# A six-layer float32 transformer block on one core: small waits rearranged, and the mixed layer's norm, index queries, top-k mask and convolution taps moved

## The chip, the cores and the metric

One core of one Trainium2 chip runs the whole program. The metric is device time in microseconds (us) of one execution. Engines: TensorE (PE) multiplies and transposes, VectorE (DVE) and ScalarE (ACT) work on SBUF and PSUM, GpSimd (POOL) on SBUF alone, and SyncE (SP) issues most of the loads. Each engine runs its own list of instructions in order, and semaphores tie the lists together.

## The reference

Four layers with post-norm (`x = layernorm(ALPHA * x + branch(x))`), their branches latent attention (MLA), windowed attention with sinks (SWA), attention with forget gates (FOX) and MLA again; then one mixed layer, a gated feed-forward (2816 wide) and a last gated projection, these with RMS norms. 512 tokens, 1024 channels, 16 heads of 64, float32 throughout. The mixed layer, on which most of the change lies:

```python
a_in, gate_c, gate_b, ...            # columns of rmsnorm(x) @ w_in
h = gate_c * a_in                    # short convolution: 3 taps over the tokens
y = gate_b * causal_depthwise_conv3(h, conv_w)
sc = relu(einsum("bqhd,bsd->bqhs", iq, ik))          # index scores, 8 heads
score = einsum("bqh,bqhs->bqs", iw, sc) * idx_scale  # masked to s <= t
_, sel = top_k(score, 128)           # keys that each query may attend to
probs = softmax(q . k * scale + bias[rel_bucket], over sel)   # 4 heads
# besides: window means (pooling), and 4 heads of full causal attention
```

All four results are concatenated and go through `w_out_2`.

## The kernel before

**Weights.** `plan_units` cuts all weights into 254 units of up to 1024 columns on 128 partitions, in the order of use. Each goes through a pipe: SyncE loads it into one of 3 raw buffers, ScalarE rounds it to fp32r (`w_hi`, `split(u)`, three units ahead of use, by `advance` or `early`), GpSimd subtracts (`w_lo`), and TensorE forms every product from three fp32r matmuls (`three`: high by high, high by low, low by high). Activations have a high part (ScalarE) and a low part (VectorE) too: `QKh/QKl`, `OTh/OTl`, `XTh/XTl`.

**Groups.** `tile(name)` on TensorE is 24 matmuls of 128x512 into bank 6 or 7; `begin` waits until the group two before has been stored. ScalarE and VectorE count the same groups (`group()`, `stored`). `place` puts a group in another bank.

**Attention.** `pair_attention` exists once on each engine and handles two heads at a time; iteration `i` runs from -2. On TensorE an iteration is `fill(i, 0)`, eight `step`s (transposes of pair `i` and scores of pair `i + 2`), `fill(i, 1)`, `fill(i, 2)`, the last scores, `mix(i)`, `fill(i, 3)`; each `fill` puts projections of later pairs there. ScalarE copies the transposes (`turned`), takes the exponentials (`exps`) and prepares weights; VectorE takes the maxima with the bias (`maxima`) and divides (`norm`). In the last iteration the first three rows of the output projection (`ahead`, `out_ahead`) are woven with the transposes (`weave`).

**Layer tails.** `out_rows` ends the output projection with the token tiles in the order 3, 2, 1, 0 (`ROWS`). VectorE's `ln_tail` makes each tile's layer norm, `turn(n)` transposes it, and ScalarE and VectorE store its halves. Work on the columns of the first tiles is opened meanwhile (`open_half`: tokens 256 to 511 of a tile of weights), and `tile` later finishes it. Before the mixed layer an RMS norm follows each layer norm (`h_norm`).

**The mixed layer.** Its units were, in this order: index keys `ik`, four index queries `iq`, six `conv`, then pool, queries, keys and values. Six `idx_block`s (four heads each, for the query tiles 1 to 3) alternate with the six convolution tiles; ScalarE takes the relu, VectorE the weighted sum into `WORK[t]`. Then `top(n)` does rounds of MAX8 and MATCH_REPLACE8: 16 for each of three query tiles, 48 in all, spread over VectorE's list. The last converts the rest into a mask in `misc`, and `maxima` adds bias and mask for pairs 2 and 3 in two passes. The convolution is done by VectorE: a product (`CONV_H`), three taps (`CONV_Y`), a product (`otmp`). GpSimd computes the window sums of the pooling.

```python
if pr.sel and t:                                     # VectorE, maxima
    link(nc.vector.tensor_tensor(pr.score(b, x, t), o, pr.bias(t, x), ALU.add))
    ins = nc.vector.tensor_tensor_reduce(pr.score(b, x, t), pr.score(b, x, t), SEL[t], ...)
```

## Time and profile before

| | |
|---|---|
| median of 3 runs | 1719.9 us (1717.58 to 1723.01) |
| profiled execution, its own time | 1719.99 us |
| span of the profile | 1718.2 us, 24228 instructions |
| TensorE busy | 1655.5 us (96%) |
| VectorE busy | 792.1 us (46%) |
| ScalarE busy | 768.3 us (45%) |
| GpSimd busy | 595.9 us (35%) |
| mean granted clock of TensorE | 0.997 |
| transfers | 161.17 MB, mean 94 GB/s |

The span goes from the first to the last instruction in the profile; the execution's own time is 1.8 us longer. TensorE's busy time and its idle time make up the span. The other engines' idle time costs nothing by itself. Layers, by TensorE: MLA to about 288 us, SWA to 478, FOX to 780, MLA to 1031, mixed to 1262, feed-forward to 1640, last projection to the end.

### The profile page before, as it was taken

How to read it: one execution, taken by the hardware profiler on the slowest of the kernel's cores; microseconds unless marked ns; L12 is line 12 of the kernel's file. 1: busy time of each engine (PE TensorE's matmuls, PEld its weight loads, DVE VectorE, ACT ScalarE, POOL GpSimd, SP SyncE). 2: the span in 40 equal slices, each digit the busy share in tenths (PEclk: the TensorE clock that was granted, in tenths of full speed). 3: DMA queues.
4: the chain of work that ended last, by engine and by line, in shares of the span. 5: the costliest groups of instructions: out<-in, count | busy, mean ns of one | idle time of the engine just before them, and what ended most of it. 6: DMA issues, size and time to landing. Idle time of an engine off the chain costs nothing.

```text
span 1718.2 us, 24228 instructions
## 1 busy us (share of the span) xinstructions
PE 1655.5 (96%) x9321; PEld 1345.2 (78%) x9321; DVE 792.1 (46%) x2055; ACT 768.3 (45%) x1565; POOL 595.9 (35%) x286
## 2 busy tenths in 40 slices
PE   7999999999999999999999998998899999999998
PEld 6777779787788787778777778776688888887877
DVE  2777626566343434426777635889332111000052
ACT  4467634566243545524566634336743222212252
POOL 4323133332243323224322224372134444444423
PEclk9999999999999999999999999999999999999999
DMA  6322144223452322144222146431143333333312
GB/s 167 68 44 62 60 148 140 76 60 66 148 155 75 84 53 77 55 152 110 58 49 76 50 142 178 106 84 53 49 147 111 98 97 95 102 95 91 123 62 86
DMA packets 216046, 161.17 MB, mean 94 GB/s; under 512 B 53755, under 2 KB 197147, under 8 KB 215932
## 3 DMA queue, kind: packets, MB, share of 16 engines
q1 hardware_dynamic: 205904, 130.21, 27.2%
q10 hardware_dynamic: 9804, 29.38, 5.5%
q8 instruction: 75, 1.23, 0.3%
q0 software_dynamic: 224, 0.03, 0.1%
q14 instruction: 39, 0.32, 0.1%
HBM read 148.32 MB, written 11.14 MB: 93 GB/s over the span
## 4 chain that ended last, share of the span: by engine, by line
PE 65%; DVE 10%; ACT 5%; issue 1%; ACTq 0%; POOL 0%; DVEq 0%
PE banks L474 18%; PE banks L476 18%; PE banks L475 18%; PE banks L717 4%; PE banks L686 3%; PE banks L732 3%; ACT AB L1434 1%; DVE misc L2555 1%; ACT G L1558 1%; DVE misc L2542 1%; DVE top L2554 1%; ACT w_hi L1304 1%; ACT AB L1460 1%; DVE QKl L1978 1%; PE banks L875 1%
## 5 line engine op out<-in xcount | busy, mean ns | idle before, releaser
L2717 POOL TENSOR_TENSOR w_lo<-w_raw,w_hi 128x1024 fp32r<-128x1024 f32 (+3 forms) x253 | 573.3, 2275 | 1095.6 <-ACT w_hi L1304 1087.4
L474 PE MATMUL banks<-XTh,w_hi 128*128 128x512 f32 (+4 forms) x1216 | 451.7, 371 | 14.3 <-DVE w_lo L2438 3.7
L475 PE MATMUL banks<-XTl,w_hi 128*128 128x512 f32 (+4 forms) x1216 | 446.0, 367 | 0.0
L476 PE MATMUL banks<-XTh,w_lo 128*128 128x512 f32 (+4 forms) x1216 | 445.8, 367 | 0.0
L1304 ACT ACTIVATE w_hi<-w_raw 128x1024 fp32r<-128x1024 f32 (+3 forms) x254 | 251.0, 996 | 154.6 <-PE banks L476 108.6
L474 PEld LDWEIGHTS banks<-XTh,w_hi 128*128 128x128 f32 (+1 forms) x1216 | 229.5, 189 | 60.4 <-issue 18.3
L476 PEld LDWEIGHTS banks<-XTh,w_lo 128*128 128x128 f32 (+1 forms) x1216 | 229.5, 189 | 38.3
L475 PEld LDWEIGHTS banks<-XTl,w_hi 128*128 128x128 f32 (+1 forms) x1216 | 229.8, 189 | 35.9
L474 PE MATMUL banks<-w_hi,OTh 128*128 128x512 f32 (+1 forms) x448 | 172.2, 384 | 1.8 <-DVE QKl L1978 1.8
L476 PE MATMUL banks<-w_hi,OTl 128*128 128x512 f32 (+1 forms) x448 | 167.8, 375 | 0.0
L475 PE MATMUL banks<-w_lo,OTh 128*128 128x512 f32 (+1 forms) x448 | 167.6, 374 | 0.0
L1460 ACT ACTIVATE AB<-banks 128x512 f32<-128x512 f32 (+1 forms) x200 | 98.7, 528 | 148.7 <-PE banks L717 146.3
L1434 ACT ACTIVATE AB<-AB,nb 128x256 f32<-128x256 f32 (+3 forms) x288 | 152.7, 537 | 13.7 <-DVE nb L2140 10.8
L2634 DVE TENSOR_TENSOR otmp<-banks,AB 128x512 f32<-128x512 f32 x22 | 15.2, 692 | 276.3 <-PE banks L476 276.3
L2130 DVE CUSTOM_DVE_ANT_0 AB<-banks,zmask 128x384 f32<-128x384 f32 (+1 forms) x192 | 83.9, 486 | 82.5 <-PE banks L717 80.0
L2159 DVE TENSOR_SCALAR_CACHE_REDUCE AB<-AB,ri 128x256 f32<-128x256 f32 (+3 forms) x256 | 118.2, 518 | 2.3
L1978 DVE TENSOR_TENSOR QKl<-banks,QKh 128x512 fp32r<-128x512 f32 (+2 forms) x80 | 54.3, 682 | 117.3 <-ACT QKh L1333 116.0
L717 PE MATMUL banks<-ident,AB 128*128 128x128 f32 x672 | 98.1, 281 | 8.6 <-ACT AB L1460 5.8
L474 PEld LDWEIGHTS banks<-w_hi,OTh 128*128 128x128 f32 x448 | 84.3, 188 | 20.2 <-DVE QKl L1978 4.0
L717 PEld LDWEIGHTS banks<-ident,AB 128*128 128x128 f32 x672 | 73.6, 141 | 29.2 <-issue 17.5
L476 PEld LDWEIGHTS banks<-w_hi,OTl 128*128 128x128 f32 x448 | 84.3, 188 | 15.4
L475 PEld LDWEIGHTS banks<-w_lo,OTh 128*128 128x128 f32 x448 | 84.4, 188 | 13.8
(204 smaller groups left out, 2322.4 us busy)
## 6 DMA issues: line engine op xcount, KB each, us to landing
w_raw<-in_w_gate_up_dram SPq DMA_DIRECT2D x44, 512.0 KB, 3.8
w_raw<-in_fox_w_in_dram SPq DMA_DIRECT2D x30, 512.0 KB, 4.1
w_raw<-in_mla_w_in_dram SPq DMA_DIRECT2D x26, 512.0 KB, 4.7
w_raw<-in_w_in_dram SPq DMA_DIRECT2D x24, 512.0 KB, 3.9
w_raw<-in_w_down_dram SPq DMA_DIRECT2D x22, 512.0 KB, 3.5
w_raw<-in_swa_w_in_dram SPq DMA_DIRECT2D x20, 512.0 KB, 3.8
w_raw<-in_mla_w_out_dram SPq DMA_DIRECT2D x16, 512.0 KB, 3.6
x_spill<-AB ACTq DMA_DIRECT2D x16, 512.0 KB, 2.8
```

What stands on the lines that cost most here:

```text
L474: nc.tensor.matmul(o, ah, bh, start=first, stop=False, skip_group_check=True)
L475: nc.tensor.matmul(o, ah, bl, start=False, stop=False, skip_group_check=True)
L476: return nc.tensor.matmul(o, al, bh, start=False, stop=last, skip_group_check=True)
L686: mm = nc.tensor.matmul(bank[2 * (c.sch % 2) + x][:, cols], qp[r, pr.q, ts], kp[r, pr.k, ks], start=n == 0 and t == pr.s_chunks[ch][0], st ...
L717: mm = nc.tensor.transpose(bank[4 + c.tch % 2][:, o:o + P], SBP[a % 2][x][:, col:col + P], ident[:, :])
L1304: nc.scalar.activation(view(w_hi, u, RING), view(w_raw, u, RAW), ACT.Copy).then_inc(hi_done, 1)
L1434: ins = nc.scalar.activation(sc, sc, ACT.Exp, bias=nb[:, b, n0 + t:n0 + t + 1], scale=pr.scale, accum_out=rs[:, b, n0 + t:n0 + t + 1])
L1460: nc.scalar.activation(PTP[x][:, pr.pt[js[0]]:pr.pt[js[0]] + width], bank[4 + c.tch % 2][:, 0:width], ACT.Copy).then_inc(pt_free, 1)
L1978: return nc.vector.tensor_tensor(dst, src, h.bitcast(F32), ALU.subtract)
L2130: ins = nc.vector.tensor_tensor_reduce(pr.score(b, x, t), o, pr.bias(t, x), 1.0, -3e38, ALU.add, ALU.max, mx[:, b, 4 * x + t:4 * x + t + 1])
L2159: ins = nc.vector.tensor_scalar(pr.score(b, x, t), pr.score(b, x, t), ri[:, b, 4 * x + t:4 * x + t + 1], None, ALU.mult, ALU.add, accum_ou ...
L2717: pool.tensor_tensor(view(w_lo, u, RING), view(w_raw, u, RAW), view(w_hi, u, RING).bitcast(F32), ALU.subtract).then_inc(lo_done, 1)
```

## The change

- Start: TensorE does 16 transposes of the identity before the first weight matmul. The seven small constants are no longer loaded by GpSimd at its start, but one behind each of its first weight preparations, the two norm gains first, with a semaphore of their own.
- SWA: the relative bias product stands between the halves of the first value projection; the query tile of pair 1 follows the first pair's scores, and the first gate precedes the second pair's.
- FOX: the rope tables of the second MLA layer are loaded in iterations 3 to 6 and not at the layer's start; ScalarE prepares a weight unit behind the next pair's first exponentials and no longer right behind the values; VectorE takes the second norm behind the mix where values follow.
- Last iteration of every attention: the remaining transpose groups are spread over four places in the second and third output row.
- Tail into the mixed layer: the third token tile's RMS norm comes ahead of the fourth tile's last passes, and its transposes ahead of the opened index-key tile; three index-query tiles are finished before the fourth tile's transposes. Loads for the pooling are issued behind the first index block.
- Convolution: product as before; the taps and the low parts are done by GpSimd between weight preparations, with `CONV_A` as its temporary.
- Attention of the mixed layer: query tiles at `fill(i, 0)` and key tiles at `fill(i, 1)`; the last values in two halves; each query tile's mask is written as NEG or 0 in fp32r (`SEL_R`) as soon as its rounds end, and TensorE adds it to the scores by a matmul with the identity. The order of the score chunks of these pairs is (2, 0), (1), (3).
- Feed-forward: of the two copies of the partial sum VectorE does one.

```diff
-    for i in range(8):
+    tile("gate", swa, D + 512)
+    tile("q", swa, 2 * P)
+    for i in range(1, 8):
...
+    for i in range(3):
+        tile("iq", w_in, iq + i * P)
     units.append(("ik", KD, HD + IDX_HEADS, [(None, 0, HD, reads(w_in, ik, ik + HD)),
...
-    for i in range(4):
-        tile("iq", w_in, iq + i * P)
+    tile("iq", w_in, iq + 3 * P)
...
             def early_mixed(turn):
-                open_half("ik")
                 for _ in range(3):
                     open_half("iq", P)
                 turn(2)
+                open_half("ik")
+                pe.wait_ge(xt_lo, c.xt)
+                for _ in range(3):
+                    tile("iq", n0=P)
                 turn(3)
...
+                    if pr.sel:                                  # TensorE, scores
+                        pe.wait_ge(ident_round, 1)
+                        pe.wait_ge(sel_done, max(pr.s_chunks[ch]))
...
+                        if pr.sel and t:
+                            for x in range(2):
+                                mm = nc.tensor.matmul(bank[2 * (c.sch % 2) + x][:, cols], ident_r[:, :], SEL_R[t],
+                                                      start=False, stop=True, skip_group_check=True)
...
                     if i == n_pairs - 1:
+                        todo = [n for n, ch in ((0, 0), (1, 1), (3, 2), (4, 0), (6, 1), (7, 2)) if ch < len(pairs[i].t_chunks)]
+                        points = [4]
...
+                    for half in range(2):
+                        half_step(k, t, half, src, begun[k], k == 0, False)
+                        if half if k == 1 else t == 0:
+                            weave()
...
             turn_start(1)
+            for _ in range(16):
+                nc.tensor.transpose(bank[0][:, 0:P], ident[:, :], ident[:, :])
             pe.wait_ge(xt_lo, 4)
...
             def fill(i, pos):                                   # TensorE, SWA
-                if pos == 0 and i == -2:
-                    pair_tile("q", 1)
-                elif pos == 1 and -1 <= i < 5:
+                if pos == 1 and i < 5:
                     pair_tile("q", i + 3)
-                elif pos == 2 and -1 <= i < 7:
+                elif (pos == 2 and 0 <= i < 7) or (pos == 0 and i == -1):
                     tile("gate")
...
+                if n == 3:                                      # ScalarE, conv tiles
+                    act.wait_ge(conv_s, 4)
...
-            pair_attention(fox_pairs(), fill)                   # VectorE
+            pair_attention(fox_pairs(), fill, FOX_VALUES)
...
+                    if t not in rounds:                         # VectorE, top
+                        nc.vector.tensor_scalar(SEL_R[t], WORK[t], TAKEN / 2, NEG, ALU.is_gt, ALU.mult).then_inc(sel_done, 1)
...
-                link(nc.vector.tensor_scalar(CONV_Y, CONV_H[:, 0:512], conv_w[:, cc, 0:1], None, ALU.mult))
-                for tap in (1, 2):
-                    link(nc.vector.scalar_tensor_tensor(CONV_Y, CONV_H[:, tap:tap + 512], conv_w[:, cc, tap:tap + 1], CONV_Y,
-                                                        ALU.mult, ALU.add))
...
+            def conv_taps(cc):                                  # GpSimd
+                pool.wait_ge(cst, N_CST)
+                groups_stored(pool, mark["conv", cc])
+                pool.tensor_scalar(CONV_Y, CONV_H[:, 0:512], conv_w[:, cc, 0:1], None, ALU.mult)
+                for tap in (1, 2):
+                    pool.tensor_scalar(CONV_A, CONV_H[:, tap:tap + 512], conv_w[:, cc, tap:tap + 1], None, ALU.mult).then_inc(conv_s, 1)
+                    pool.wait_ge(conv_s, 4 * cc + 2 * tap - 1)
+                    pool.tensor_tensor(CONV_Y, CONV_Y, CONV_A, ALU.add).then_inc(conv_s, 1)
+                    pool.wait_ge(conv_s, 4 * cc + 2 * tap)
```

VectorE, tail into the mixed layer, from the third token tile's layer norm on, before (`banks` holds the layer's output, `HT` tiles lie in `AB`):

```order
L2250 SCALAR_TENSOR_TENSOR banks<-AB,banks 128x1024
L2251 BN_STATS st<-banks 128x6
L2252 BN_STATS st<-banks 128x6
L2253 BN_AGGR mv<-st 128x2
L2256 SCALAR_TENSOR_TENSOR banks<-banks,mv,AB 128x1024
L2017 RECIPROCAL inv<-dev 128x1
L2258 SCALAR_TENSOR_TENSOR AB<-banks,inv,AB 128x1024
L2017 RECIPROCAL inv<-dev 128x1
L2237 SCALAR_TENSOR_TENSOR AB<-AB,inv,V 128x1024
L2017 RECIPROCAL inv<-dev 128x1
L2237 SCALAR_TENSOR_TENSOR AB<-AB,inv,V 128x1024
L2223 TENSOR_TENSOR XTl<-banks,XTh 128x4x128 x4
```

and now:

```order
L2314 SCALAR_TENSOR_TENSOR banks<-AB,banks 128x1024
L2315 BN_STATS st<-banks 128x6
L2316 BN_STATS st<-banks 128x6
L2317 BN_AGGR mv<-st 128x2
L2091 RECIPROCAL inv<-dev 128x1
L2301 SCALAR_TENSOR_TENSOR AB<-AB,inv,V 128x1024
L2323 SCALAR_TENSOR_TENSOR banks<-banks,mv,AB 128x1024
L2091 RECIPROCAL inv<-dev 128x1
L2325 SCALAR_TENSOR_TENSOR AB<-banks,inv,AB 128x1024
L2287 TENSOR_TENSOR XTl<-banks,XTh 128x4x128 x2
L2091 RECIPROCAL inv<-dev 128x1
L2301 SCALAR_TENSOR_TENSOR AB<-AB,inv,V 128x1024
```

The RMS norm of the third tile (the first pass with `V`, the gain) has moved ahead of the fourth tile's two last passes, and the third tile's low part ahead of the fourth's norm.

GpSimd, the mixed layer's start, before (`L2717` is the weight preparation, `L2697` begins the window sums):

```order
L2717 TENSOR_TENSOR w_lo<-w_raw,w_hi 128x576
L2717 TENSOR_TENSOR w_lo<-w_raw,w_hi 128x1024 x14
L2697 TENSOR_TENSOR AB<-AB 128x512 x2
L2705 TENSOR_TENSOR AB<-AB,V 64x512
L2706 TENSOR_TENSOR AB<-AB 64x512
L2705 TENSOR_TENSOR AB<-AB,V 64x512
L2706 TENSOR_TENSOR AB<-AB 64x512
L2717 TENSOR_TENSOR w_lo<-w_raw,w_hi 128x1024 x3
L2697 TENSOR_TENSOR AB<-AB 128x512 x4
```

and now:

```order
L2817 TENSOR_TENSOR w_lo<-w_raw,w_hi 128x576
L2817 TENSOR_TENSOR w_lo<-w_raw,w_hi 128x1024 x6
L2800 TENSOR_SCALAR AB<-AB,conv_w 128x512
L2802 TENSOR_SCALAR AB<-AB,conv_w 128x512
L2804 TENSOR_TENSOR AB<-AB 128x512
L2802 TENSOR_SCALAR AB<-AB,conv_w 128x512
L2804 TENSOR_TENSOR AB<-AB 128x512
L2817 TENSOR_TENSOR w_lo<-w_raw,w_hi 128x1024 x2
L2810 TENSOR_TENSOR OTl<-otmp,OTh 128x512
L2817 TENSOR_TENSOR w_lo<-w_raw,w_hi 128x1024
L2800 TENSOR_SCALAR AB<-AB,conv_w 128x512
L2802 TENSOR_SCALAR AB<-AB,conv_w 128x512
```

Of the ten tap operations the first five and the first low part are seen between weight preparations; the window sums moved behind the second five.

VectorE, mixed attention, from the last top-k round to the maxima of pair 2, before:

```order
L2554 MAX top<-misc 128x8
L2555 MATCH_REPLACE misc<-top,misc 128x512
L2615 TENSOR_SCALAR misc<-misc 128x1152
L2155 RECIPROCAL ri<-rs 128x4 x2
L2126 TENSOR_TENSOR AB<-banks,G 128x384
L2127 ISA AB,mx<-AB,misc 128x384
L2127 ISA mx 128x1
L2130 ISA AB,mx<-banks,G 128x128
L2130 ISA mx 128x1
```

and now:

```order
L2634 MAX top<-misc 128x8
L2635 MATCH_REPLACE misc<-top,misc 128x512
L2637 TENSOR_SCALAR OTh<-misc 128x512
L2052 TENSOR_TENSOR QKl<-banks,QKh 128x512
L2199 ISA AB,mx<-banks,G 128x384
L2199 ISA mx 128x1
L2199 ISA AB,mx<-banks,G 128x128
L2199 ISA mx 128x1
```

The conversion of all three tiles became one of the last tile, the low part of a query tile stands ahead of the maxima, the wait for pair 1's exponentials (the two RECIPROCAL) is no longer ahead of them, and one pass over the scores replaces two.

## Rows read from the trace of the kernel before

**Rows 1.** view of waits, TensorE, whole span: engine, line, releaser, us in total, times, longest

```profile
PE banks L875 <- DMA AB<-in_x_dram: 6.1, 2, 5.2
...
PE banks L474 <- DVE G L2363: 0.3, 2, 0.2
```

**Rows 2.** TensorE in order of time, start: start us, us, engine, line, operation, [idle before]

```profile
8.06 1.97 PE L875 MATMUL banks<-ident,AB 128*128 128x128 f32 x8 [0.90 <-DMA AB<-in_x_dram]
13.77 0.55 PE L474 MATMUL banks<-XTh,w_hi 128*128 128x256 f32 x1 [3.74 <-DVE w_lo L2438]
...
18.12 0.28 PE L476 MATMUL banks<-XTh,w_lo 128*128 128x256 f32 x1
...
21.36 0.28 PE L476 MATMUL banks<-XTh,w_lo 128*128 128x256 f32 x1
```

**Rows 3.** view of waits, TensorE, 298 to 316 us

```profile
PE banks L686 <- DVE mx L2130: 2.0, 2, 1.6
PE banks L474 <- ACT V_odd L1760: 1.2, 1, 1.2
```

**Rows 4.** TensorE in order of time, mixes of last pairs

```profile
228.97 2.38 PE L732 MATMUL banks<-AB,V_odd 128*64 128x512 f32 x16 [0.83 <-ACT AB L1460]
...
437.88 1.74 PE L732 MATMUL banks<-AB,V 128*64 128x256 f32 x16 [0.67 <-ACT AB L1460]
```

**Rows 5.** TensorE in order of time, third layer

```profile
492.77 0.47 PE L474 MATMUL banks<-XTh,w_hi 128*128 128x512 f32 x1 [1.26 <-ACT AB L1793]
...
705.14 0.36 PE L474 MATMUL banks<-w_hi,XTh 128*128 128x256 f32 x1 [0.84 <-DVE G L2011]
...
719.10 1.11 PE L717 MATMUL banks<-ident,AB 128*128 128x128 f32 x6 [1.34 <-ACT AB L1460]
```

**Rows 6.** ScalarE in order of time, behind the third layer's last values

```profile
717.42 1.05 ACT L1304 ACTIVATE w_hi<-w_raw 128x1024 fp32r<-128x1024 f32 x1
```

**Rows 7.** busy by stretch: PE, PEld, DVE, ACT, POOL with counts; clock, DMA, GB/s

```profile
722.00:723.00 1.00, 1.00 (x4) 0.71 (x4) 0.55 (x1) 1.00 (x4) 0.00 (x0) 0.50 0.81 262
...
1186.00:1187.00 1.00, 1.00 (x7) 0.67 (x6) 0.97 (x3) 0.39 (x1) 0.00 (x0) 0.50 0.00 0
```

**Rows 8.** view of waits, TensorE, 1035 to 1072 us

```profile
PE banks L1119 <- DVE QKl L1978: 1.4, 1, 1.4
PE banks L875 <- DVE AB L2237: 1.4, 2, 0.8
```

**Rows 9.** view of waits, TensorE, 1110 to 1150 us

```profile
PE banks L474 <- DVE otmp L2577: 1.6, 1, 1.6
PE banks L1128 <- issue: 0.5, 1, 0.5
```

**Rows 10.** view of waits, TensorE, 1150 to 1243 us

```profile
PE banks L686 <- DVE QKl L1978: 4.1, 2, 2.4
PE banks L732 <- DVE QKl L1978: 2.8, 1, 2.8
PE banks L717 <- ACT AB L1460: 2.5, 3, 1.5
PE banks L717 <- ACT AB L1449: 1.7, 1, 1.7
```

**Rows 11.** VectorE's line of the index sums: duration ns min/median/max, first and last start

```profile
L2542 DVE SCALAR_TENSOR_TENSOR misc<-AB,iw_t,misc x21: 483/619/2724, 1072.7 to 1116.4; 128x256 f32<-128x256 f32 x7, 128x384 f32<-128x384 f32 x7, 128x512 f32<-128x512 f32 x7
```

**Rows 12.** GpSimd's groups by shape: busy us, mean ns, idle before

```profile
L2697 POOL TENSOR_TENSOR AB<-AB 128x512 f32<-128x512 f32 x6 | 6.5, 1081 | 0.6 <-issue 0.3
...
L2678 POOL COPY w_raw<-w_raw 128x128 f32<-128x128 f32 x2 | 0.6, 287 | 1.0 <-DMA w_raw<-in_mla_w_in_dram 1.0
```

**Rows 13.** VectorE's groups by shape, 1035 to 1053 us

```profile
L2258 DVE SCALAR_TENSOR_TENSOR AB<-banks,inv,AB 128x1024 f32<-128x1024 f32 x2 | 2.6, 1284 | 0.1
```

**Rows 14.** VectorE in order of time, last selection

```profile
1192.81 0.76 DVE L2615 TENSOR_SCALAR misc<-misc 128x1152 f32<-128x1152 f32 x1
```

**Rows 15.** TensorE in order of time, second feed-forward part

```profile
1552.46 0.50 PE L474 MATMUL banks<-XTh,w_hi 128*128 128x512 f32 x1 [1.18 <-ACT V L1944]
```

327 lines of the change are left out of this document (198 added, 129 removed).

## The prediction

> **What bounds the kernel now.** I read the page first, then the view of waits of TensorE over the whole span, then TensorE's rows in order of time around every wait above 0.2 us, and only then the other engines around those places. TensorE is busy nearly throughout; its waits are small and many. The view of waits has 24 groups, from 6.1 us down to 0.3 us [rows 1], and they sum to 56.3 us of a 1718.2 us span. So this kernel's time is TensorE's work plus this list, and a change that removes no TensorE work can return at most some 56 us plus what a low clock costs. The reader is to see that no single wait matters, and that the change must be priced wait by wait.
>
> Three more stretches are slow without a wait: right after the waits at 719, 1052 and 1185 us the granted clock is 0.50, TensorE's lower level [rows 7] (the first and the last of the three). Each lasted 3.4 us at half speed, so each cost 1.7 us. In each case TensorE had stood still for 1.6 us or more within the few microseconds before it [rows 5, 8, 10]; but other waits of this size are not followed by one, so the clock's part is less sure than the waits.
>
> **The change, part by part.** I go along the span; gains are positive.
>
> Start. The first weight matmul begins at 13.77 us after 3.74 us of idling, and the first 20 matmuls take (18.12 - 13.77) / 20 = 0.218 us each, the later ones (21.36 - 18.12) / 27 = 0.120 us [rows 2]: 20 x 0.098 = 1.9 us. The 16 added transposes go into the idle stretch. Eight took 1.97 us there [rows 2], so 16 need 3.5 to 3.9 us against a gap of 3.74 us: they fill it and may overrun by 0.2. I take 1.8. Bounds: -0.3 (they overrun and the clock is no higher) to 2.9 (the constants' transfers, no longer beside the first tokens, also give a microsecond). The moved DMA issues stand behind weight preparations on GpSimd's queue; the gains are needed only in the latent scaling and the others in the second layer.
>
> Second layer. The two matmuls of the relative bias now stand between the halves of the value projection: of the 1.2 us wait on their copy [rows 3] 0.2 should stay. The 2.0 us before the second pair's scores [rows 3] get a query tile and a gate tile as cover. But the second query tile is then directly before the first transposes: the next scores need its low half (about 1.5 us after the tile), and VectorE divides the first pair's second half (1.9 us) only behind it. I expect 0.8 and 1.1 us of new wait there, so this cover gives nothing net. Sum 1.0; bounds -1 to 3.
>
> Third layer. Eight rope-table issues leave ScalarE's queue ahead of the value copies: 1.26 us go [rows 5] (its first row). They return two at a time where ScalarE waits for matmuls anyway. VectorE now normalises behind the mix where values follow: the gate tile's wait of 0.84 goes. In the 1.34 us wait after the last values ScalarE did a weight split of 1.05 us ahead of the copy that TensorE waited for [rows 5, 6]; it now comes after: 1.0. With it the low clock behind it should go, 1.7. Sum 4.8; bounds 2.1 to 5.1.
>
> Last pair of each layer. The last two transpose groups stood back to back ahead of the mix, which waited 0.83 us in four layers and 0.67 in the windowed one [rows 4]. Now six output matmuls stand behind the last transposes: 4 x 0.83 + 0.67 = 4.0; bounds 2 to 4.
>
> Tail into the mixed layer. Before, TensorE waited 1.4 us for the two normalised token tiles and 1.4 us for the index queries [rows 8]. Now the third tile's norm runs ahead of two passes of 1.28 us each [rows 13] over the fourth, so it is ready about 2.8 us earlier; but TensorE also comes 2.9 us earlier, since one opened tile (24 matmuls at 0.12) now stands behind that turn: about 0.9 of wait, and 0.1 for its low half. The wait on the fourth tile's low half stays, for nothing is between its turn and its use. The second 1.4 go, because three query tiles end a tile earlier and ScalarE's five DMA issues stand behind the first index block. So 2.8 becomes 1.0: 1.8, and 1.7 for the clock: 3.5; bounds 0 to 5.
>
> Convolution and pooling. VectorE loses two taps and a low part per half; GpSimd gains three TENSOR_SCALAR and two TENSOR_TENSOR of 512 columns. The latter take 1.08 us; a COPY of a quarter of the columns took 0.28 [rows 12], so a TENSOR_SCALAR lies between 0.3 and 1.1; I take 1.0, near the row of equal width: 5.2 us per half. What counts is VectorE's accumulations beside it. They take 0.48 us at best and 2.72 at worst [rows 11]; the worst spans a weight preparation on GpSimd: an operation with both inputs in SBUF stands still meanwhile, while the top-k operations do not.
> The Trainium skill, "SBUF — State Buffer" (section "SBUF: two separate sides"), says that VectorE and GpSimd share a port pair as an exclusive lock, and the loser "fully blocks". By that rule each tap operation can hold up an accumulation; the trace agrees, with the 2.72 us above.
> From the stretched accumulations alone I count only part of the taps' use: idle sum before 1.6 [rows 9] + 0.5 for the pool product + 0.3 = 2.4. After: 0.7 before the fifth index block (ScalarE's relu waits for the convolution product behind three top-k rounds), 1.3 where 1.6 was, 1.5 for the pool product, whose GpSimd chain has one low part of 1.08 more ahead, 0.4 for the second: 3.9. So -1.5; bounds -9 (rival A) to 2.4. Queued behind GpSimd's new waits is the preparation of the next weights, needed only two tiles of 5.6 us later.
>
> Mixed attention. The waits were 4.1, 2.8, 2.5 and 1.7 = 11.1 us [rows 10]. Each of the first got a projection tile as cover: query tiles are now before the scores and key tiles behind. The 2.8 (a bank held by VectorE's late low part behind the masked maxima) goes, for that part is now ahead of the maxima; the 1.7 goes with the exponentials done first under the second value half. The next late thing is ScalarE after the first mix, about 1.0, and the six transposes of the third pair in a row, about 1.3. So 11.1 - 2.3 = 8.8. The mask costs TensorE 12 matmuls, 4 x (256 + 384 + 512) = 4608 columns at 0.12 us per 256: -2.1. Low clock gone: 1.7. VectorE's last selection ended at 1192.81 + 0.76 [rows 14]; scores of 512 keys now wait for it. By the order after it should come some 3 us before TensorE asks, so nothing; without that margin every microsecond counts in full. Sum 8.4; bounds 2 to 12.
>
> Feed-forward. One of the two copies goes to VectorE, so they overlap: of 1.18 [rows 15] 0.4 goes.
>
> Sum: 1.8 + 1.0 + 4.8 + 4.0 + 3.5 - 1.5 + 8.4 + 0.4 = 22.4 us. The profiled execution took 1719.99 us, the median of the runs shown is 1719.9, so both give 1697.6.
>
> **The rivals.**
> A. GpSimd's taps hold VectorE up as its weight preparations do. Ten tap operations of 1.08 us can hold VectorE for 10.8 us; 1.5 are counted. For it: accumulations did stretch to 2.72 us. Against: VectorE has idle time before index blocks, and the top-k rounds are unaffected. If 7 more reach TensorE: 1704.6.
> B. The low clock stays or falls in new places, as in the second layer where I foresee two new waits within 3 us. Three such stretches: 22.4 - 5.1 = 17.3, so 1702.7.
> C. The waits that I added (1.9 second layer, 3.9 convolution, 2.3 attention) come out mostly hidden; 6 of 8.1 us less: 1691.6.
> D. Slower: GpSimd's TENSOR_SCALAR with a scale per partition is far slower than the rows allow me to think; no row shows one. Six stand in a chain whose product holds ScalarE's relu and so the next index block. Each microsecond above 1.0 costs six, so above 4.7 us each the whole gain is gone. At 6 us: 1697.6 + 30 = about 1727.
> E. The change moves waits rather than removing them, and nothing is left: ScalarE and VectorE are each half idle and their order alone decides the rest; a new wait behind each removed one gives 1718.
>
> **How the numbers follow.** Forecast 0.58, A 0.18, B 0.08, C 0.09, D 0.04, E 0.03. What a measurement here can tell from no change is 0.3%, 5.2 us. Forecast, A, B and C are faster by more: 0.93; E is the same: 0.03; D is slower: 0.04. The range takes in A, B and C with their spread: below, 1689, since every bound above together is unlikely; above, 1709, where A and B meet. Outside it lie D, E and a little of A.
>
> **What would show it.** Start: the matmuls from about 13.8 us are 0.12 apart. Waits before the mixes of the last pairs are gone; in the third layer no wait above 0.5 us between 485 and 745. Granted clock 1.0 behind the third layer's last values and between 1040 and 1190. GpSimd's TENSOR_SCALAR at about 1 us (D falls above 2). A new wait in the second layer before the third pair's scores, and waits of 3 to 4 us in the convolution. The scores of 512 keys with a mask start without waiting for VectorE. I am wrong if the waits' sum stays above 40 us, if the mask's matmuls are far longer than 0.24 us, or if weights come late.

## The result, and the profile after

The changed kernel takes 1699.1 us (1696.4 to 1700.9, four runs), the kernel before 1720.8 us in the same comparison: ratio 0.9877, interval 0.9862 to 0.9891. That is 21.8 us less; the forecast was 1697.6, in a range of 1689 to 1709. A second set of runs of the same changed kernel gave 1699.3 us (1697.1 to 1701.1), ratio 0.9882 (0.9864 to 0.9900).

| | before | after |
|---|---|---|
| profiled execution | 1719.99 us | 1696.41 us |
| span | 1718.2 us | 1694.3 us |
| TensorE busy | 1655.5 us | 1654.3 us |
| sum of TensorE's waits, by the view of waits | 56.4 us | 33.4 us |
| VectorE busy | 792.1 us | 785.9 us |
| GpSimd busy | 595.9 us | 613.0 us |

The profiled execution is the fastest of the four. TensorE does the same work plus 12 mask matmuls and the 16 transposes of the start, and its waits sum to 23.0 us less: the time is again its work plus its waits.

TensorE's waits over the whole span of the changed kernel (line waited for, releaser, us in total, times, longest; 13 groups left out) answer to [rows 1]:

```profile
PE banks L905 <- DMA AB<-in_x_dram: 5.2, 1, 5.2
PE banks L739 <- ACT AB L1510: 3.5, 9, 0.6
...
PE banks L905 <- DVE AB L2301: 2.1, 3, 1.1
PE banks L481 <- DVE XTl L2287: 2.0, 3, 1.6
PE banks L1133 <- DVE QKl L2052: 1.8, 1, 1.8
...
PE banks L1161 <- issue: 1.7, 1, 1.7
...
PE banks L481 <- DVE otmp L2654: 0.3, 1, 0.3
```

Of before, the waits at L686 and L732 (4.1 and 2.8 us, [rows 10]) and the one of 1.6 on `otmp` [rows 9] are gone or small. Two are not: the 1.4 us at the index scores (L1119, [rows 8]) are 1.8 now, at the small transposes ahead of them (L1133), and the 0.5 at the pool product (L1128, [rows 9]) are 1.7 (L1161). What is left in one piece are the first tokens (5.2 us), the tail into the mixed layer (1.1 + 1.6 + 1.8 us) and the pool product (1.7 us).

The start, TensorE in order of time, answers to [rows 2]. The first weight matmul begins 1.96 us earlier, and the next ones are 0.12 us apart at once:

```profile
8.62 2.07 PE L1019 MATMUL banks<-ident 128*128 128x128 f32 x16
11.81 0.36 PE L481 MATMUL banks<-XTh,w_hi 128*128 128x256 f32 x1 [1.12 <-DVE w_lo L2515]
12.01 0.28 PE L482 MATMUL banks<-XTl,w_hi 128*128 128x256 f32 x1
```

Granted clock (the third number from the right) in the changed kernel, against [rows 7]. While TensorE works, one low stretch is left, in the tail (a second one begins at 1691.7 us, behind the last matmul); where the third of before was, it is 1.00:

```profile
1047.00:1050.00 3.00, 3.00 (x16) 3.00 (x15) 1.11 (x2) 1.51 (x3) 3.00 (x2) 0.50 0.50 117
1185.00:1189.00 4.00, 3.47 (x31) 2.58 (x28) 1.47 (x5) 2.74 (x7) 0.00 (x0) 1.00 0.00 0
```

How far each part moved TensorE's work, read as the start of the same matmuls in both profiles (before minus after, then the difference from one place to the next):

| part | places (before / after, us) | forecast | measured |
|---|---|---|---|
| start | 41.63 / 37.80 | 1.8 | 3.8 |
| rest of the first layer | 256.46 / 251.70 | 0.8 | 0.9 |
| second layer | 464.74 / 457.73 | 1.7 | 2.3 |
| third layer | 769.76 / 756.70 | 5.6 | 6.0 |
| fourth layer, tail, to the first index scores | 1071.06 / 1057.20 | 4.3 | 0.8 |
| convolution, to the first pool product | 1131.42 / 1117.39 | -1.5 | 0.2 |
| mixed attention, to the feed-forward's start | 1285.87 / 1262.29 | 9.2 | 9.5 |
| feed-forward | 1552.46 / 1528.47 | 0.4 | 0.4 |
| sum | | 22.4 | 23.9 |

(The last pairs' 4.0 us are spread over the layers where they lie.) Two rows are off by 2 us or more, in opposite ways (start and tail), and the convolution by 1.7; the sum hides that.

The tail, TensorE in order of time: the third token tile's transposes, the fourth's, the index keys behind them, and the small transposes ahead of the first index scores.

```profile
1031.73 1.09 PE L905 MATMUL banks<-ident,AB 128*128 128x128 f32 x8 [1.05 <-DVE AB L2301]
...
1043.74 1.06 PE L905 MATMUL banks<-ident,AB 128*128 128x128 f32 x8
1046.37 0.34 PE L481 MATMUL banks<-XTh,w_hi 128*72 128x256 f32 x1 [1.57 <-DVE XTl L2287]
...
1056.95 0.32 PE L1133 MATMUL banks<-ident,AB 8*128 8x8 f32 x3 [1.83 <-DVE QKl L2052]
```

GpSimd's groups by shape (busy us, mean ns, idle before), against [rows 12]: a TENSOR_SCALAR takes 1.71 us where 1.0 was taken, a tap's addition 1.34.

```profile
L2802 POOL TENSOR_SCALAR AB<-AB,conv_w 128x512 f32<-128x512 f32 x4 | 6.8, 1712 | 0.2
L2779 POOL TENSOR_TENSOR AB<-AB 128x512 f32<-128x512 f32 x6 | 6.5, 1084 | 0.3
L2804 POOL TENSOR_TENSOR AB<-AB 128x512 f32<-128x512 f32 x4 | 5.4, 1341 | 0.3
...
L2800 POOL TENSOR_SCALAR AB<-AB,conv_w 128x512 f32<-128x512 f32 x2 | 3.5, 1730 | 5.3 <-DVE AB L2646 3.1 <-issue 2.2
```

VectorE's accumulations of the index scores, against [rows 11]:

```profile
L2622 DVE SCALAR_TENSOR_TENSOR misc<-AB,iw_t,misc x21: 483/750/2778, 1059.2 to 1097.6; 128x256 f32<-128x256 f32 x7, 128x384 f32<-128x384 f32 x7, 128x512 f32<-128x512 f32 x7
```

By shape their sum rose from 17.2 us (6.3 + 5.6 + 5.3) to 21.7 us (7.7 + 7.6 + 6.4). Little of this stands beside the taps: the four accumulations that overlap a tap operation are longer than their shape's shortest by 0.9 us and three times 0.24 us, 1.6 us in all. The four that overlap a weight preparation are longer by 7.1 us (before: two, by 4.2 us).

### The profile page after: what moved, and what is told of

Same layout as the page of the kernel before. It is cut to its first block, busy times and chain, and to the rows that moved or that the text cites. A ratio compares the mean times of both kernels' runs of the same rounds, so it can differ in the third digit from the quotient of the medians.

```text
span 1694.3 us, 24289 instructions
## 1 busy us (share of the span) xinstructions
PE 1654.3 (98%) x9349; PEld 1343.5 (79%) x9349; DVE 785.9 (46%) x2038; ACT 767.5 (45%) x1565; POOL 613.0 (36%) x298
## 4 chain that ended last, share of the span: by engine, by line
PE 81%; DVE 9%; ACT 6%; issue 2%; POOL 1%; DMA 0%; ACTq 0%; SPq 0%; DVEq 0%; POOLq 0%
PE banks L481 22%; PE banks L483 22%; PE banks L482 22%; PE banks L739 5%; PE banks L700 4%; PE banks L754 4%; PE banks L905 1%; PE banks L723 1%; ACT G L1613 1%; ACT AB L1484 1%; ACT w_hi L1354 1%; DVE misc L2622 1%; DVE AB L2228 1%; POOL w_lo L2817 1%; DVE QKl L2052 1%
## 5 line engine op out<-in xcount | busy, mean ns | idle before, releaser
L2817 POOL TENSOR_TENSOR w_lo<-w_raw,w_hi 128x1024 fp32r<-128x1024 f32 (+2 forms) x253 | 572.3, 2271 | 1050.6 <-ACT w_hi L1354 1039.4
L481 PE MATMUL banks<-XTh,w_hi 128*128 128x512 f32 (+5 forms) x1216 | 450.7, 371 | 7.2 <-DVE XTl L2287 2.0
L483 PE MATMUL banks<-XTh,w_lo 128*128 128x512 f32 (+5 forms) x1216 | 444.7, 366 | 0.0
L482 PE MATMUL banks<-XTl,w_hi 128*128 128x512 f32 (+5 forms) x1216 | 444.7, 366 | 0.0
L1354 ACT ACTIVATE w_hi<-w_raw 128x1024 fp32r<-128x1024 f32 (+4 forms) x254 | 250.3, 995 | 160.3 <-PE banks L483 107.7
L481 PEld LDWEIGHTS banks<-XTh,w_hi 128*128 128x128 f32 (+2 forms) x1216 | 228.2, 188 | 53.2 <-issue 11.2
L483 PEld LDWEIGHTS banks<-XTh,w_lo 128*128 128x128 f32 (+2 forms) x1216 | 228.2, 188 | 38.1
L482 PEld LDWEIGHTS banks<-XTl,w_hi 128*128 128x128 f32 (+2 forms) x1216 | 228.4, 188 | 36.1 <-issue 0.2
```

The costliest lines, as they stand in the source:

```text
L481: nc.tensor.matmul(o, ah, bh, start=first, stop=False, skip_group_check=True)
L482: nc.tensor.matmul(o, ah, bl, start=False, stop=False, skip_group_check=True)
L483: return nc.tensor.matmul(o, al, bh, start=False, stop=last, skip_group_check=True)
L1354: nc.scalar.activation(view(w_hi, u, RING), view(w_raw, u, RAW), ACT.Copy).then_inc(hi_done, 1)
L2817: pool.tensor_tensor(view(w_lo, u, RING), view(w_raw, u, RAW), view(w_hi, u, RING).bitcast(F32), ALU.subtract).then_inc(lo_done, 1)
```

## Experiments

Each is the changed kernel with one thing undone or added, unless said; medians beside 1699.1 and 1699.3 us.

**Is the low clock fixed in its places?** The changed kernel once more, without an edit.

> The changed kernel once more, unchanged, beside the next two, as their measure. Its first profile has a wait of 1.83 us before the index scores and a low clock behind the 1.57 us wait before it; five variants that leave this place alone show 2.9 to 3.3 us there and the low clock behind it, and three runs show a low clock at 320 us that it does not have. Theory: these two places change from execution to execution (the low clock of 1.7 us falls or does not), which is the spread of 1696.4 to 1700.9: here one of them or both differ from the first profile. Rival: they are fixed, and the variants' edits made them: the profile repeats 1.83 us and no low clock at 320 and 1060 us.

Measured: 1699.3 us, and another profile, of the slowest of its runs (1701.1 us, span 1699.0). The low clock now lies at 321.3 to 324.7 us and at 1058.6 to 1065.4 us, and no longer at 1046.6 to 1050.0:

```profile
322.00:323.00 1.00, 1.00 (x10) 0.78 (x7) 0.00 (x0) 0.00 (x0) 0.00 (x0) 0.50 0.07 19
1059.00:1060.00 1.00, 1.00 (x10) 0.98 (x11) 0.32 (x2) 0.19 (x1) 1.00 (x1) 0.50 1.10 236
1063.00:1064.00 1.00, 1.00 (x4) 0.81 (x3) 0.00 (x0) 0.00 (x0) 0.00 (x0) 0.50 1.08 269
```

```profile
1048.00 0.34 PE L481 MATMUL banks<-XTh,w_hi 128*72 128x256 f32 x1 [1.57 <-DVE XTl L2287]
...
1058.67 0.45 PE L1133 MATMUL banks<-ident,AB 8*128 8x8 f32 x3 [3.26 <-DVE QKl L2052]
```

So the same kernel has low stretches in other places from execution to execution, and the wait ahead of the index scores is 3.3 us where no low clock stood before it: in the first profile the 3.4 us at half speed had brought TensorE there 1.4 us later. From the 1.57 us wait to the small transposes it is 10.6 us in the first profile and 10.7 in the second, so the low stretch between them cost next to nothing: the wait behind it became shorter by what it took. The theory holds. Elsewhere a stretch of 3.4 or 6.8 us costs up to half of its length. The profile of 1694.3 us was a lucky one: its execution is the fastest of the eight of this kernel, and two profiles of the same kernel differ by 4.7 us of span. A forecast from one profiled execution (three stretches) to another has an uncertainty of some 2 us from this, either way, by my estimate.

**The start, two runs.** `after_cold` leaves out the 16 transposes; `before_warm` is the kernel before with them alone.

```diff
-            for _ in range(16):
-                nc.tensor.transpose(bank[0][:, 0:P], ident[:, :], ident[:, :])
```

> The changed kernel without its 16 transposes at the start. The start gained 3.8 us where 1.8 was forecast: the first weight matmul begins 1.96 us earlier, and its matmuls are 0.12 instead of 0.22 us apart. Theory: two independent parts, the earlier begin from the constants' transfers that no longer stand beside the first tokens, the spacing from the transposes. Then here the first weight matmul still begins at about 11.8 us, about 19 matmuls are 0.21 us apart, and the time is 1.9 us more than the changed kernel's 1699.1: 1701.0. Rival: with the idling cut from 3.7 to some 3 us the matmuls come at full speed by themselves: spacing 0.12 from the start, 1699.

> The kernel before with nothing but the 16 transposes. Theory: the first weight matmul begins at 13.8 us as before (the transposes fit into the idling), its matmuls are 0.12 us apart, gain 1.9 us: 1718.9 against 1720.8. Rival: the transposes end some 1.6 us before the weights are there, TensorE stands still again, and the first matmuls are 0.21 us apart as before: no gain, 1720.8.

Measured: `after_cold` 1701.6 us, `before_warm` 1719.2 against 1720.7 us (ratio 0.9992, 0.9981 to 1.0003, by itself not told from no change). The profiles tell what the times can't. Without the transposes, the first weight matmul still begins at 11.9 us, and the first 22 take 4.82 us, 0.22 each; from there 0.12:

```profile
11.90 0.55 PE L481 MATMUL banks<-XTh,w_hi 128*128 128x256 f32 x1 [2.98 <-DVE w_lo L2513]
...
16.51 0.37 PE L481 MATMUL banks<-XTh,w_hi 128*128 128x256 f32 x1
...
17.08 0.28 PE L482 MATMUL banks<-XTl,w_hi 128*128 128x256 f32 x1
```

In the kernel before with them, the first weight matmul begins at 13.61 us, 2.15 us after the last transpose, and its followers are 0.12 us apart:

```profile
9.55 1.91 PE L989 MATMUL banks<-ident 128*128 128x128 f32 x16
13.61 0.36 PE L474 MATMUL banks<-XTh,w_hi 128*128 128x256 f32 x1 [2.15 <-DVE w_lo L2440]
```

Both theories hold for the transposes: they give 1.9 to 2.1 us. The earlier first matmul does not come from them; of the other edits only the constants' transfers lie ahead of it, but no run moves them alone. Nor does a pause of 2.15 us bring the low speed back there. The other traces bear this out: in each, the clock's own record begins, at full speed, where the matmuls' spacing halves. That is at 18.1 and 16.7 us in the two without the transposes, and at 8.5 to 12.0 us in the twelve with them. The moment differs from execution to execution, so the transposes themselves took 1.9 to 3.3 us; in `before_warm` the speed had risen at 9.24 us, just before them, and they kept TensorE at work in what had been a pause of 3.74 us.

**The last pairs.** `after_no_weave` puts the transpose groups back to back again.

```diff
-                        todo = [n for n, ch in ((0, 0), (1, 1), (3, 2), (4, 0), (6, 1), (7, 2)) if ch < len(pairs[i].t_chunks)]
-                        points = [4]
...
-                            if len(todo) >= points[0]:
+                            if todo:
                                 step(i, todo.pop(0))
...
-                        if half if k == 1 else t == 0:
-                            weave()
+                    weave()
```

> The changed kernel with the last pairs' transposes as before (back to back behind the first rows, ahead of the mix). Theory: the waits before the mixes return, 0.83 us in four layers and 0.67 in the windowed one, 4.0 us in all: 1703.1. Rival: the waits were only put elsewhere, and the woven order has cost something of its own: waits return but others go, under 2 us: 1700.

Measured: 1703.9 us (1703.7 to 1704.1). TensorE's waits of this line were 0.6 us in the changed kernel; here, 0.83 us four times and 0.67 once beside it:

```profile
PE banks L754 <- ACT AB L1505: 4.6, 6, 0.8
```

4.0 us came back in this view, as the theory says; the medians are 4.6 to 4.8 us apart, so up to a microsecond lies elsewhere.

**The third layer.** `after_fox_early_split` prepares the weight unit right behind the values again.

```diff
-                elif pos == 5 and i - 1 in FOX_VALUES:
-                    advance()
-                    early()
...
-                        advance()
-                        for half in range(2):
-                            values(half, FOX_VALUES[i] % 2)
+                        value_units(FOX_VALUES[i] % 2)
```

> The changed kernel, but in the third layer ScalarE prepares the next weight unit right behind the values again, ahead of the copy of transposes that TensorE waits for. Theory: the wait behind the last values grows from 0.39 to about 1.4 us, the granted clock falls to 0.50 behind it for 3.4 us (1.7 us of cost): 2.7 us more than 1699.1: 1701.8. Rival: only the wait returns and the clock stays at 1.00, since the two never hung together: 1700.1. Second rival: the exponentials that are now ahead of it cover the preparation: no change.

Measured: 1700.6 us. The wait is back, 1.34 instead of 0.39 us, and behind it the clock is low from 711.7 to 715.1 us:

```profile
709.52 1.60 PE L739 MATMUL banks<-ident,AB 128*128 128x128 f32 x10 [1.34 <-ACT AB L1510]
```

```profile
713.00:714.00 1.00, 1.00 (x4) 0.81 (x3) 0.50 (x1) 1.00 (x5) 0.00 (x0) 0.50 0.93 369
```

In this layer the two cost 2.5 us (633.92 to 759.35 us here, 633.77 to 756.70 in the changed kernel). The theory holds by the profile. The median moved by 1.2 to 1.5 us only. The other low stretches can explain the rest: the mean granted clocks of its four executions average 0.9978, those of the changed kernel 0.9970 and 0.9973, which at 1700 us is an estimated 0.9 to 1.3 us in this variant's favour.

**The taps.** `after_dve_taps` gives them back to VectorE; ScalarE's wait for them goes too.

```diff
+                groups_stored(dve, c.g)
+                link(nc.vector.tensor_scalar(CONV_Y, CONV_H[:, 0:512], conv_w[:, cc, 0:1], None, ALU.mult))
+                for tap in (1, 2):
+                    link(nc.vector.scalar_tensor_tensor(CONV_Y, CONV_H[:, tap:tap + 512], conv_w[:, cc, tap:tap + 1], CONV_Y,
+                                                        ALU.mult, ALU.add))
                 idx_block(3 * cc + 2)
...
-                dve.wait_ge(conv_s, 4 * cc + 4)
...
-                if u in (conv0 + 4, conv0 + 7):
-                    conv_taps((u - conv0 - 4) // 3)
```

> The changed kernel with the convolution's taps done by VectorE again (product, then TENSOR_SCALAR and two accumulations, ahead of the third index block of each half); the low parts stay with GpSimd. VectorE gets 7.3 us of work back. In the changed kernel the last selection ends at 1177.2 us and the scores of 512 keys start at 1179.4: 2.2 us of slack. Theory: taps on GpSimd are worth what they take off VectorE ahead of the last selection: a part falls into VectorE's idle time, the selection ends 3 to 6 us later and TensorE waits 1 to 4 us before the scores of 512 keys; waits of 1 to 2 us before the index blocks return: 1703 (1700 to 1706). Rival A of the prediction: GpSimd's taps stretch VectorE's accumulations (21.7 us in sum against 17.2 before), so that VectorE gains little; with the taps back they are short again and the time is 1698 to 1700.

Measured: 1706.1 us (1706.0 to 1707.2), 0.1 us above the theory's range, and not by its path. TensorE did not wait for the selection; it waited in the convolution (view of waits, 1070 to 1136 us), with a low clock behind each wait:

```profile
PE banks L481 <- DVE otmp L2656: 2.5, 1, 2.5
PE banks L1152 <- ACT AB L1940: 2.3, 1, 2.3
```

```profile
1093.00:1094.00 1.00, 1.00 (x4) 0.83 (x3) 1.00 (x1) 0.89 (x2) 1.00 (x1) 0.50 0.00 0
1117.00:1118.00 1.00, 1.00 (x4) 0.81 (x3) 0.93 (x4) 0.97 (x2) 1.00 (x1) 0.50 0.00 0
```

2.3 + 2.5 + 0.4 us in place of 0.3 + 1.7 are 3.2 us more, two low stretches 3.4: together 6.6, of 6.8 measured. (Its other two low stretches, at 321 and 1058 us, stand in the second profile of the changed kernel as well.) So the taps on GpSimd are worth 6.8 us in the changed kernel. That is not a gain over before: this row of the table moved by 0.2 us. Between the convolution's two products VectorE now does six and four top-k rounds where it did one; without the taps moved, the new order would have cost some 6.6 us here (an estimate, 6.8 less 0.2). Rival A of the prediction is right in a small part: the accumulations sum to 19.1 us here (9.2 + 6.5 + 3.4) against 21.7. Of these 2.6 us some 1.6 stood beside the taps; the rest is weight preparations that meet other accumulations. VectorE is rid of 7.3 us by the taps, and no wait shows that the 1.6 us reached TensorE. Rival D is out: at 1.71 us a TENSOR_SCALAR stands far below the 4.7 us from which it would have decided.

**The mask.** `after_dve_mask` adds it on VectorE in a second pass.

```diff
-                            for x in range(2):
-                                mm = nc.tensor.matmul(bank[2 * (c.sch % 2) + x][:, cols], ident_r[:, :], SEL_R[t],
-                                                      start=False, stop=True, skip_group_check=True)
...
+                                link(nc.vector.tensor_tensor(pr.score(b, x, t), o, pr.bias(t, x), ALU.add))
+                                ins = nc.vector.tensor_tensor_reduce(pr.score(b, x, t), pr.score(b, x, t), SEL_R[t].bitcast(F32), 1.0, -3e38,
```

> The changed kernel with the top-k mask added by VectorE again, in a second pass over the scores (12 more passes), without the mask's 12 matmuls and without TensorE's wait for the selection. Theory: TensorE gives back 2.1 us, but the maxima of the last two pairs come 2 to 3 us later each and TensorE waits for exponentials and banks: 1702 (1699 to 1705). Rival: the new order of the query and key tiles did it all, and the mask on TensorE is a pure loss of 2.1 us: 1697.

Measured: 1701.6 us. TensorE is rid of 2.1 us of matmuls and waits 2.77 us for VectorE's maxima before the scores of 512 keys, 1.03 us where it was 0.46, and 1.7 us go to a low clock from 1184.0 to 1187.4 us:

```profile
1183.02 0.50 PE L700 MATMUL banks<-QKh 64*128 64x512 f32 x2 [2.77 <-DVE mx L2198]
...
1191.04 1.11 PE L732 MATMUL banks<-ident,AB 128*128 128x128 f32 x6 [1.03 <-ACT AB L1503]
```

2.8 + 0.6 + 1.7 - 2.1 = 3.0 us, where 2.3 to 2.6 were measured. The mask on TensorE pays, by some 2 us net. The rest of the 9.5 us I put down to the order, to the last pair (0.8) and to the low clock that is gone (1.7); no run undoes the order by itself.

**The tail, four runs.** `tail_turn` moves the fourth tile's transposes ahead of the third finished query tile:

```diff
-                for _ in range(3):
+                for _ in range(2):
                     tile("iq", n0=P)
                 turn(3)
+                tile("iq", n0=P)
```

> The changed kernel with the fourth token tile's transposes ahead of the third of the finished index-query tiles and no longer behind it. In the changed kernel that tile's norm is ready at 1037.4 us and its transposes start at 1043.7; TensorE then waits 1.57 us for its low half and the clock is 0.50 for 3.4 us. Theory: the query tile of 2.7 us covers the low half, the wait and the low clock both go: 1.6 + 1.7 = 3.3 us less than 1699.1: 1695.8. Rival: the wait goes but the clock falls behind the next wait of this size (1.83 us, ten us later): 1697.5.

Measured: 1695.6 us (1693.7 to 1695.9). The 1.57 us went, and so did the low clock in the tail; but the wait ahead of the index scores is 2.92 us:

```profile
1056.10 0.32 PE L1134 MATMUL banks<-ident,AB 8*128 8x8 f32 x3 [2.92 <-DVE QKl L2053]
```

`best1` has this edit and two more: ScalarE's copy of the index keys ahead of `advance()`, and `conv_low(1)` behind `window_sums(0)`.

```diff
             act.wait_ge(xt_lo, c.xt)
-            advance()
             o = group()
...
+            advance()
...
-                elif u in (conv0 + 6, conv0 + 9):
-                    conv_low((u - conv0 - 6) // 3)
+                elif u == conv0 + 6:
+                    conv_low(0)
                 if u == pool0 + 3:
                     window_sums(0)
+                    conv_low(1)
```

> The changed kernel with three edits: the fourth token tile's transposes ahead of the third finished index-query tile; ScalarE copies the index keys ahead of the weight preparation that it now does first (it waits there until 1052.5 us while the keys are ready at 50.8); GpSimd does the second low part of the convolution behind the window sums, for whose result TensorE waits 1.71 us. Theory: 3.3 us for the first, 1.8 for the second (the wait before the first index block), 1.3 for the third (one low part): 6.4 us less than 1699.1: 1692.7. Rival: the waits at the index block and at the pool product are set by VectorE's low parts and by the window sums' own length, and only the first edit pays: 1695.8.

Measured: 1695.2 us, no more gained than by `tail_turn`: the rival's time. The keys are now there in time (1052.49 us, no wait), and the wait stands one group further on, 2.56 us:

```profile
1052.49 0.35 PE L1134 MATMUL banks<-ident,AB 8*128 8x8 f32 x3
...
1056.30 0.59 PE L481 MATMUL banks<-XTh,w_hi 128*128 128x512 f32 x1 [2.56 <-DVE QKl L2053]
```

So the keys' copy alone was not the cause. The third edit did shorten the first pool product's wait, from 1.71 to 0.50 us, but 0.74 us came up at the second, so 0.5 us is left of the 1.3 expected. ScalarE's weight preparations waited for loads. SyncE's own rows in the changed kernel show why: it issues four loads from 1020 to 1027 us, stands until 1046.4 us at `wait_ge(xt_lo, mark["mixed"])`, the last token tile's low part, and then puts four bias rows, 1.8 to 2.0 us together, ahead of each load:

```profile
1020.12 6.97 SPq L1327 DMA_DIRECT2D w_raw<-in_w_in_dram  x4
1046.41 1.76 SPq L1311 DMA_DIRECT2D G<-rel_scratch  x4
1048.22 0.42 SPq L1327 DMA_DIRECT2D w_raw<-in_w_in_dram  x1
1048.69 1.97 SPq L1311 DMA_DIRECT2D G<-rel_scratch  x4
```

The load of 1048.22 us landed at 1052.42 and is what ScalarE prepares at 1052.49, ahead of the keys' copy:

```profile
1052.49 1.06 ACT L1354 ACTIVATE w_hi<-w_raw 128x1024 fp32r<-128x1024 f32 x1 [3.98 <-issue]
1053.58 0.59 ACT L1926 ACTIVATE AB<-banks 8x512 f32<-8x512 f32 x1
```

`bias_late` is the changed kernel with that wait and the bias rows two units later, and nothing else:

```diff
-                if u == conv0:
+                if u == conv0 + 2:
                     sp.wait_ge(rel_dma, 16 * 8)
                     sp.wait_ge(xt_lo, mark["mixed"])
-                if conv0 <= u < conv0 + 8:
-                    bias_rows(u - conv0)
+                if conv0 + 2 <= u < conv0 + 10:
+                    bias_rows(u - conv0 - 2)
```

> The changed kernel, but SyncE's wait for the last token tile's halves, and the 32 issues of bias rows that stand between its weight loads, come two weight units later. In the changed kernel SyncE stands from 1027 to 1046.4 us at that wait, the next weight load is issued at 1048.2 us and ScalarE's preparation of it, at 1052.5, holds up the copy of the index keys. Theory: that load is what the 1.8 to 3.3 us before the index scores wait for: they go (to under 0.5 us), the 1.57 us stay: 2 to 4 us less, 1696 (1695 to 1697.5). Rival: the keys' own copies (0.6 + 1.2 us on ScalarE, 1.4 on VectorE) behind 4 us of cover set it: nothing changes, 1699.

Measured: 1694.9 us (1694.3 to 1695.5), 4.2 to 4.5 us less and 0.1 us below the theory's range. SyncE issues six loads before the first bias row, the one that was held back now at 1028.2 us, and no wait above 0.45 us is left between 1047 and 1115 us; the 1.57 us and the low clock behind it stay:

```profile
1020.21 29.54 SPq L1327 DMA_DIRECT2D w_raw<-in_w_in_dram  x6
1049.87 1.89 SPq L1311 DMA_DIRECT2D G<-rel_scratch  x4
```

The theory holds: a load that SyncE held back is what the wait ahead of the index scores hung on. In the kernel before SyncE stood at the same place. Its first bias rows and the load behind them, which landed at 1058.4 us, are shown here; whether its own wait of 1.4 us hung on that load, no run shows.

```profile
1052.61 1.75 SPq L1261 DMA_DIRECT2D G<-rel_scratch  x4
1054.40 0.43 SPq L1277 DMA_DIRECT2D w_raw<-in_w_in_dram  x1
```

**All together.** `best2` joins `best1` and `bias_late`, and swaps the first gate with the third query tile of the second layer.

```diff
-    tile("gate", swa, D + 512)
     tile("q", swa, 2 * P)
+    tile("gate", swa, D + 512)
...
-                if pos == 1 and i < 5:
+                if (pos == 1 and i < 5 and i != -1) or (pos == 0 and i == -1):
                     pair_tile("q", i + 3)
```

> All together on the changed kernel: the fourth token tile's transposes ahead of the third finished index-query tile; the index keys' copy ahead of the weight preparation; SyncE's wait and bias rows two units later; GpSimd's second low part behind the window sums; and in the second layer the third query tile ahead of the first gate, so that its low half is not needed right behind it (0.77 and 0.87 us of waits there, with a low clock of 1.7 us in some runs). Theory: before the index scores no wait above 0.5 us, no low clock between 1030 and 1070 us: 3.3 + 2.5 us; pool product 1.2; second layer 1.2 and the low clock: 8 us less than 1699.1: 1691. Rival: in the tail the earlier finish only meets the next thing (best1 turned 1.57 + 1.83 us into 2.56 us and gained no more than its first edit alone): 1694 to 1695.

Measured: 1693.3 us (1691.7 to 1694.6). In the tail no wait is left between the fourth tile's transposes and the index scores, and no low clock, as the theory says; the 1.1 us before the third tile's transposes stay. At the pool products 1.7 us became 0.5 + 0.7, a gain of 0.5 where 1.2 was expected. The swap went wrong: 0.77 + 0.87 us became one wait of 2.52 us, with a low clock behind it.

```profile
321.23 0.66 PE L740 MATMUL banks<-ident,AB 128*128 128x128 f32 x4 [2.52 <-DVE AB L2229]
```

`best3` is `best2` without the swap.

> The last kernel without its edit in the second layer (the gate goes ahead of the third query tile again, as in the changed kernel): there the waits of 0.77 and 0.87 us had become one of 2.52 us with a low clock behind it. What stays are the four edits of the tail and the convolution. Theory: 0.9 us less than 1693.3 by the waits, and up to 1.7 more where no low clock falls at 320 us: 1692 (1691 to 1693). Rival: the low clock at 320 us falls behind 0.77 and 0.87 us as well, as in some runs of the changed kernel, and the tail's gain is the whole: no difference that can be told from 1693.3.

Measured: 1691.2 us (1690.8 to 1692.8), ratio to before 0.9837 (0.9819 to 0.9855): 8 us below the changed kernel, 29 below the one before. The 0.77 and 0.87 us are back, and this execution has no low stretch before TensorE's last matmul. It is 2.1 us below `best2`, of which 0.9 are the waits; but the two were measured in different comparisons and their ranges touch, so how much the low clock at 320 us adds is not shown. The largest waits left between 1018 and 1140 us:

```profile
PE banks L906 <- DVE AB L2302: 1.1, 1, 1.1
PE banks L1162 <- POOL AB L2789: 0.7, 1, 0.7
PE banks L1162 <- issue: 0.5, 1, 0.5
```

## Why the prediction was right, and where it was wrong

*Bound by TensorE's work and its waits*: right. Waits 23.0 us less, low stretches 3.4 (three against one) and the start's low speed 1.9 less, the mask 2.1 and the 16 transposes 2.1 more: 24.1, of 23.9 measured.

*Start*: too small, 3.8 against 1.8, outside its upper bound of 2.9. The transposes gave what was said (1.9 to 2.1: `after_cold` by its profile and its median, `before_warm` by its profile). They did not fill the gap, though: the price of 3.5 to 3.9 us was taken from transposes at the low speed, and here they took 2.07 us, since the speed rose among them. The moved constants were given at most "a microsecond" and gave 1.96: before, the second token tile came 0.9 us late [rows 2] and ScalarE waited 0.65 us more for the first weights, whose preparation began at 11.31 us; in the changed kernel neither waits and it begins at 9.36.

*Second layer*: right in its parts, 2.3 against 1.7; of the wait on the copy nothing stayed, where 0.2 were left. The new waits of 0.77 and 0.87 us stand where 0.8 and 1.1 were forecast, and there the low clock falls in some executions, as rival B had it.

*Third layer*: right, 6.0 against 5.6 with the last pair's. The clock's share, of which I was less sure, came back in `after_fox_early_split`'s profile together with the wait.

*Last pairs*: right, 4.0 us by the waits that come back when they are undone.

*Tail*: wrong. The step that failed is "the second 1.4 go, because three query tiles end a tile earlier and ScalarE's five DMA issues stand behind the first index block". 3.5 us were forecast and nothing came (6.08 us of waits and clock before, 6.15 after). The issues on ScalarE were not what was last: a weight load was, held back by SyncE's wait for the last token tile, which I had not looked up in SyncE's own rows. `bias_late` moved that wait and the bias rows behind it, and gave 4.2 to 4.5 us. The first part of the step (0.9 us of wait before the third tile) came as 1.05, and the wait on the fourth tile's low part stayed as said, but so did the low clock behind it, which the forecast had let go.

*Convolution*: better than forecast, 0.2 against -1.5. GpSimd's operations cost more (1.71 and 1.34 us for 1.0 and 1.08), the chain of a half is 7.8 us for 5.2, yet the waits forecast ahead of the fifth index block (0.7), of the convolution product (1.3) and of the second pool product (0.4) came as 0, 0.3 and 0; only the first pool product's did, 1.7 for 1.5. I had left out that VectorE, rid of 7.3 us, reaches its product earlier than the longer chain is late: at the first product it did not wait for GpSimd, at the second 0.46 us.
The Trainium skill, "GPSIMD Engine Reference" (section "3.1 Elementwise — side-by-side cycle accounting"), gives 769 ns as the best case of a loop over 512 elements and puts TENSOR_TENSOR above it, for its two inputs. Here it is the other way: 1.71 us with one input and a scale per partition (1.55 the shortest), 1.08 us with two inputs [rows 12], and the measurement decides.

*Mixed attention*: right in sum, 9.5 against 9.2 with the last pair's 0.8. The waits left are 0.46, 0.39, 0.29 and 0.56 us, 1.7 where 2.3 were forecast. The margin of the selection was 3.0 us, as estimated: VectorE's last selection began at 1176.79 us and took 0.43, and TensorE needs it only for the mask behind the scores of 512 keys, at 1180.26 (the expectation of `after_dve_taps`, which says 2.2, counts to the scores themselves):

```profile
1176.79 0.43 DVE L2637 TENSOR_SCALAR OTh<-misc 128x512 fp32r<-128x512 f32 x1
```

```profile
1179.37 0.50 PE L700 MATMUL banks<-QKh 64*128 64x512 f32 x2
...
1180.26 0.73 PE L717 MATMUL banks<-OTh,ident_r 128*128 128x512 f32 x2
```

*Rivals*: A is out as a loss, though the accumulations did grow by 4.5 us, 1.6 of them beside taps. B was partly true: low stretches still fall, one of 3.4 us in the first profile of the changed kernel, 3.4 and 6.8 us in the second. The eight executions of this kernel take 1696.4 to 1701.1 us, and the forecast of 1697.6 lies within them. That the sum came so near is partly luck: the start's 2.0 and the convolution's 1.7 us more than forecast made up for the tail's 3.5 less. C was partly true: of the 8.1 us of new waits 5.3 came (1.6 in the second layer, 2.0 in the convolution, 1.7 in the attention). D and E are out.

## What to carry to other kernels

Price a change by the list of single waits and the low clock behind them, but for each wait follow all queues that feed it, the load queue's own waits too: a wait that was put down to VectorE's copy hung on a weight load that SyncE had held back for 19 us. A cover removes a wait only when nothing else is nearly as late; `best1` moved the wait one group further, at 2.6 us, and gained nothing by it until the load was early. And a low stretch that lies ahead of a wait is paid for by that wait; only one with no wait close behind it costs its half. Compare low-clock stretches between two profiles before crediting their difference to the edit.

## What was not expected of the hardware

- The low clock of 3.4 us behind a wait is not fixed: behind the same 1.57 us wait it fell in one execution and not in another of the same kernel, and it fell behind waits of 0.77 and 0.87 us, 1.8 us apart, in some executions and not in others.
- In the first microseconds the granted clock in the profile's views reads 1.00 while the matmuls are 0.21 us apart (11.9 to 16.7 us in `after_cold`). The trace has no clock record before 16.70 us there, and the views print 1.00 where there is none; only the spacing shows the low speed.
- TensorE had done nothing but transposes when its spacing halved, from 0.21 to 0.11 us, in all twelve traces that have the 16 at the start (at 8.94 us in the changed kernel).
- GpSimd's TENSOR_SCALAR with a scale per partition (1.71 us for 128x512) is slower than its TENSOR_TENSOR of the same width (1.08 to 1.34 us).
- An accumulation on VectorE that met a tap operation of 1.3 to 2.0 us on GpSimd grew by 0.24 to 0.9 us; one that met a weight preparation of 2.4 us grew by 1.0 to 2.2 us.
